# A hybrid decoder step on one core: order of VectorE work at the MoBA gates, order of the operand split, place of the memory transposes

## The reference, cut to what matters

```python
u = jax.nn.sigmoid(g_m) * (h_m @ W['w_proj_m']) + jax.nn.sigmoid(g_a) * (h_a @ W['w_proj_a'])
x = x + u @ W['w_out']
...
# memory_kv: mem is (1, 256, 2048), the keys and values of the cross attention
mn = rms_norm(mem, norm_mem)
return (mn @ w_xk), (mn @ w_xv)
```

## Time and profile before

| | us |
|---|---|
| median of 3 runs | 2289.93 |
| the three runs | 2280.73, 2289.93, 2290.65 |
| the profiled execution | 2281.03 |
| its span, first to last instruction | 2279.5 |
| TensorE busy in the span | 2130.7 (93%) |
| VectorE busy | 1206.3 (53%) |
| ScalarE busy | 797.3 (35%) |
| mean granted TensorE clock | 0.959 |

### The profile page before, as it was taken

One profiled execution on the slowest core, in us unless ns is written; L12 is line 12 of the kernel. 1 busy time (PEld: TensorE's weight loads), 2 busy tenths in 40 slices (PEclk: granted clock), 3 DMA queues, 4 the chain that ended last, 5 costly groups with the idle time before them and its releaser, 6 DMA issues.

```text
span 2279.5 us, 40609 instructions
## 1 busy us (share of the span) xinstructions
PE 2130.7 (93%) x16438; PEld 2009.2 (88%) x16438; DVE 1206.3 (53%) x1424; ACT 797.3 (35%) x1010; POOL 63.5 (3%) x85
## 2 busy tenths in 40 slices
PE   4999997998999999898899877999999999999997
PEld 4989896998778788888899756999999999999997
DVE  4354465343556465656446535666564456666444
ACT  3333332343333333323234333333333333333333
POOL 0011011010000000000000000000000000000000
PEclk7999997999999999999899988999999999999999
DMA  7145434454686876554444451454545555454543
GB/s 244 47 151 175 150 105 140 132 175 145 216 315 244 306 273 219 176 163 147 164 143 157 162 185 37 148 175 157 168 134 173 158 180 183 147 176 144 171 154 115
DMA packets 305491, 384.78 MB, mean 169 GB/s; under 512 B 6146, under 2 KB 278690, under 8 KB 304626
## 3 DMA queue, kind: packets, MB, share of 16 engines
q1 hardware_dynamic: 300530, 365.72, 48.9%
q0 software_dynamic: 4896, 18.13, 2.5%
HBM read 370.94 MB, written 12.88 MB: 168 GB/s over the span
## 4 chain that ended last, share of the span: by engine, by line
PE 87%; DVE 6%; ACT 3%; issue 2%; SPq 1%; DMA 1%; DVEq 0%; POOL 0%; PEldq 0%; ACTq 0%; PEld 0%; POOLq 0%
PE bank L1699 19%; PE bank L1700 19%; PE bank L1703 18%; PE bank L1713 8%; PE bank L1717 6%; PE bank L2158 4%; PE bank L2157 4%; PE bank L2162 4%; ACT w_hi L639 1%; DVE w_lo L1046 1%; PE bank L1710 1%; DVE n_tmp L1078 1%; PE bank L1939 1%; PE bank L1938 1%; PE bank L1942 1%
## 5 line engine op out<-in xcount | busy, mean ns | idle before, releaser
L1699 PE MATMUL bank<-xn_hi,w_hi 128*128 128x288 f32 x3152 | 882.8, 306 | 69.1 <-DVE xn_lo L1086 26.1
L1046 DVE TENSOR_TENSOR w_lo<-raw,w_hi 128x2048 fp32r<-128x2048 f32 (+2 forms) x289 | 605.0, 2096 | 616.7 <-ACT w_hi L639 614.0
L1700 PE MATMUL bank<-xn_lo,w_hi 128*128 128x288 f32 x3152 | 874.1, 303 | 0.0
L639 ACT ACTIVATE w_hi<-raw 128x2048 fp32r<-128x2048 f32 (+2 forms) x289 | 503.9, 1745 | 694.1 <-PE bank L1703 476.7
L1699 PEld LDWEIGHTS bank<-xn_hi,w_hi 128*128 128x128 f32 x3152 | 614.5, 195 | 83.5 <-issue 45.0
L1700 PEld LDWEIGHTS bank<-xn_lo,w_hi 128*128 128x128 f32 x3152 | 614.1, 195 | 0.1
L1703 PE MATMUL bank<-xn_hi,w_lo 128*128 128x288 f32 x3152 | 450.2, 295 | 0.0
L1703 PEld LDWEIGHTS bank<-xn_hi,w_lo 128*128 128x128 f32 x3152 | 429.5, 189 | 0.0
L2157 PE MATMUL bank<-f_hi,w_hi 128*128 128x288 f32 x704 | 191.4, 296 | 0.0
L2158 PE MATMUL bank<-f_lo,w_hi 128*128 128x288 f32 x704 | 190.8, 297 | 0.0
L2157 PEld LDWEIGHTS bank<-f_hi,w_hi 128*128 128x128 f32 x704 | 132.5, 188 | 0.1
(11 more groups left out here) (363 smaller groups left out, 1762.1 us busy)
## 6 DMA issues: line engine op xcount, KB each, us to landing
raw<-w_in_dram SPq DMA_DIRECT2D x44, 2048.0 KB, 9.0
raw<-w_ffn_gate_dram SPq DMA_DIRECT2D x22, 2048.0 KB, 8.1
raw<-w_ffn_up_dram SPq DMA_DIRECT2D x22, 2048.0 KB, 8.1
raw<-w_ffn_down_dram SPq DMA_DIRECT2D x32, 1408.0 KB, 6.6
raw<-cache_k_dram SPq DMA_DIRECT2D x64, 512.0 KB, 5.4
raw<-cache_v_dram SPq DMA_DIRECT2D x64, 512.0 KB, 5.3
raw<-w_out_dram SPq DMA_DIRECT2D x8, 2048.0 KB, 8.6
w_pm_raw<-w_proj_m_dram SPq DMA_DIRECT2D x8, 1024.0 KB, 5.6
```

Of the source, the lines that this page charges most:

```text
L639: nc.scalar.activation(like(wh[ph.half(c)], src), src, ACT.Copy).then_inc(hi_ready, 1)
L1046: nc.vector.tensor_tensor(like(wl[ph.half(c)], src), src, like(wh[ph.half(c)], src).bitcast(F32), ALU.subtract).then_inc(slot_read[ph.slot ...
L1699: mm(out, wh[half][:, k, :], rh[:, k, 0:n], start=k == 0, stop=False)
L1700: mm(out, wh[half][:, k, :], rl[:, k, 0:n], start=False, stop=False)
```

## The change

Three things are moved; no arithmetic is added or removed.

1. `ga_tail` frees the bank right after the multiplication, and stands ahead of `lo` of the same j.
2. At the end of the gates ScalarE splits quarters 0 to 2 of u before it converts the first weight tile of `p_wo`, and VectorE's order becomes: quarters 0 and 1, `ga_tail` of half tile 0, quarter 2, `ga_tail` of half tile 1, first `w_lo`, quarter 3.
3. The memory transposes are made in two groups of 16, one between tiles 2 and 3 and one after tile 3 of the first iteration of `p_wo`; the copies stand between weight conversions, and the loop over the next two iterations is written out.

```diff
 # ScalarE
-            hi(p_wo, 0, 0, 0, src256(p_wo.slot(0), 0))
             for q in range(4):
                 act.wait_ge(x_u, 4 * q + 5)
                 a_copy(xh[:, 4 * q:4 * q + 4, :], U2[:, 4 * q:4 * q + 4, :]).then_inc(x_uhi, 1)
+                if q == 2:
+                    hi(p_wo, 0, 0, 0, src256(p_wo.slot(0), 0))
...
-            for n in (0, 2, 4, 6):
+            def mem_copy(n):
...
-            with act.Fori(1, 3) as i:
-                for j in range(4):
-                    hi(p_wo, i, j // 2, j, src256(p_wo.slot(j // 2), j % 2))
+            for j in range(4):
+                if j < 2:
+                    mem_copy(4 * j)
+                    mem_copy(4 * j + 2)
+                hi(p_wo, 1, j // 2, j, src256(p_wo.slot(j // 2), j % 2))
+            for j in range(4):
+                hi(p_wo, 2, j // 2, j, src256(p_wo.slot(j // 2), j % 2))
 # VectorE
                 dc.run(nc.vector.tensor_tensor(ut[:], G[p_ga.bank(2 + j)][:, 0:NT], sg[:, j, :], ALU.mult))
+                nc.vector.engine_nop().then_inc(evac_done[p_ga.bank(2 + j)], 1)
                 dc.sync()
                 nc.vector.tensor_tensor(U2[:, ds(i * 2 + j, 1), :], U[:, ds(i * 2 + j, 1), :], ut[:].unsqueeze(1), ALU.add).then_inc(x_u, 1)
-                nc.vector.engine_nop().then_inc(evac_done[p_ga.bank(2 + j)], 1)
...
                     if not first:
+                        ga_tail(i - 1, j)
                         lo(p_ga, i, 0, j, src256(p_ga.slot(0), j))
-                        ga_tail(i - 1, j)
...
-            lo(p_wo, 0, 0, 0, src256(p_wo.slot(0), 0))
-            for q in range(4):
-                if q == 3:
-                    ga_tail(7, 0)
-                    ga_tail(7, 1)
+            def u_lo(q):
                 dve.wait_ge(x_uhi, q + 1)
...
+            u_lo(0)
+            u_lo(1)
+            ga_tail(7, 0)
+            u_lo(2)
+            ga_tail(7, 1)
+            lo(p_wo, 0, 0, 0, src256(p_wo.slot(0), 0))
+            u_lo(3)
...
+            for j in range(4):
+                if j < 2:
+                    mem_copy(4 * j + 1)
+                    mem_copy(4 * j + 3)
+                lo(p_wo, 1, j // 2, j, src256(p_wo.slot(j // 2), j % 2))
+                add_to_x(p_wo, (0, 1)[j // 2], (j + 2) % 4, (j + 2) % 4, ds(2 + j, 1))
+            wo_body(2, False)
 # TensorE
+            for j in range(4):
+                tile(p_wo, 0, j // 2, j, j, x_sem=None if j else x_ulo)
+                if j == 2:
+                    pe.wait_ge(landed[2], p_min.landed(0, 0))
+                if j >= 2:
+                    for n in range(4 * j - 8, 4 * j - 4):
+                        mem_rows(n)
             pe.drain().then_inc(slot_read[2], 1)
-            with pe.Fori(1, 3) as i:
+            for i in range(1, 3):
                 for j in range(4):
                     tile(p_wo, i, j // 2, j, j)
```

More of the change, by code:

```diff
@@ L1462, in wo_body, with mem_copy @@
                         add_to_x(p_wo, i - 1, j + 2, j + 2, ds(i * 4 + (j - 2), 1))
-            wo_body(0, True)
-            for n in (1, 3, 5, 7):
+            def mem_copy(n):
                 dve.wait_ge(tp_done, 9 + n + 1)
@@ L1468, in _ @@
                                       B[2 + n % 4][:].rearrange("p (k c) -> p k c", c=P)).then_inc(tp_odd, 1)
-            with dve.Fori(1, 3) as i:
-                wo_body(i, False)
+            wo_body(0, True)
+            for j in range(4):
[5 more added lines that the diff above has]
+            wo_body(2, False)
             def mem_lo(j):
@@ L2020, in _, with mem_rows @@
                 ga_body(i, False)
[L2021 to L2026, removed]
+            def mem_rows(n):
                 t, k4 = n // 4, n % 4
```

## The result

The changed kernel takes 2251.07 us (median of 4 runs, 2247.76 to 2252.39), before beside it 2287.1 (4 runs, 2280.73 to 2290.65): ratio 0.9841, 95% interval 0.9817 to 0.9865, or 36 us (31 to 42). The forecast was 2250, range 2241 to 2264.

The account below looks back on a forecast made before the run. TensorE, busy 93% of the span, bounds it: only its idle or low-clock time can be won. Gates 24.3, projection start 2.2 and transposes 7.2 make 33.7 off 2281.03: 2247 or 2256, forecast 2250, own range 2243 to 2260, wider 2241 to 2264.

Parts of the forecast that it names:

- Gates: Gate stage: with the tail first, the stalls at the iteration edges go; 24.3 us less in all.
- stalls 16.5, clock 5.9 and refill 1.9: Gate stage's sum: TensorE's waits gone, four iterations back from granted clock 0.93, six restarts after a stall saved.
- the second rival: Gates and projection: the clock swings without the stalls, 5.9 + 1.5 + 1.2 us stays, 2256 us; chance 8%.
- the multiplication starts at E - 1.5, right behind the reciprocal: VectorE at a gate edge: multiplication starts 1.5 us before the second half tile's end and takes 0.45.
- The bank is free at E - 1.0: Gate edge: bank released 1.0 us before TensorE ends the second half tile, so the stall goes.
- The weights' cover: Gates' next `w_in` transfer: 3 us of cover for a median transfer, thinnest of the change, costed at nothing.
- The rival of the weights: Gates: shorter iterations find `w_in` missing, 21 us given back, 2268 us at the lower level; chance 12%.
- Start of the projection: Output projection's first tile: TensorE starts 4.2 us earlier but waits for quarter 3; 2.2 us less taken.
- the clock's term: Projection's start: gain 2.7 us if the clock stays up, 1.2 if two new gaps lower it, costing 1.5.
- Memory transposes: Output projection: two groups remove 4.74 us idle and 2.73 of clock and refill, 0.3 added; 7.2 us less.
- The loop: Output projection: writing the loop out costs nothing, since straight-code tiles already stand 6.39 us apart.
- The level: Whole kernel: runs lie on two levels some 9 us apart, so 2247 or 2256 us, equally likely.

Follow-up runs that it names:

- Experiment 1: The kernel before with only the gates' tail order and early bank release changed; ratio 0.9887, median 2262.44 us.
- experiment 2: The kernel before with only the bank's release moved right behind the multiplication, low weights still ahead of the tail; ratio 0.9949, median 2277.2 us.
- experiment 3: The changed kernel with the bank's release put behind the addition again; ratio 0.9867, median 2254.07 us.
- experiment 7: The changed kernel with the next gate weights' transfer held until VectorE has read the first half of the half tiles' weights; median 2259.59 us.
- experiment 6: The changed kernel with TensorE's loop over two iterations of the output projection kept as a loop; ratio 0.9849, median 2251.22 us.
- experiment 4: The kernel before with only the split of u while products run; ratio 0.9971, median 2282.74 us.
- experiment 5: The kernel before with only the memory transposes in two groups of 16, copies between weight conversions; ratio 0.998, median 2283.09 us.
- experiment 9: The changed kernel with VectorE's order at the projection's start: tail 0, quarter 0, tail 1, quarters 1 to 3, low weights last; 2247.75 us, one run.
- experiment 10: The changed kernel with u's low quarter 0 on GpSimd and VectorE's order tail 0, quarter 1, tail 1, quarters 2 and 3, low weights; ratio 0.9832.
- experiment 8: The changed kernel with u's low quarters 0 and 1 made by GpSimd and both tails ahead of VectorE's part of the split; median 2250.1 us.

## Why the prediction was right, point by point

**Gates: 24.3 forecast, 24.22 measured.** Experiment 1 shows that part 1 does it alone. The split into stalls 16.5, clock 5.9 and refill 1.9 is borne out for the clock by experiment 2, where the same instructions with shorter gaps won 5.9 beyond the stalls. (Six times 0.33 is 2.0, not 1.9; what the measured 24.2 leaves beside stalls and clock is 1.8.) "If the low clock of four iterations isn't caused by the gap", the premise of the second rival, is false. The step that failed in a detail is "the multiplication starts at E - 1.5, right behind the reciprocal". The same edge in the changed kernel, VectorE, TensorE and SyncE:

```profile
943.19 1.96 DVE L1343 RECIPROCAL x_gates<-x_gates 128x288 f32<-128x288 f32 x1
945.66 0.46 DVE L1427 TENSOR_TENSOR x_tmp<-bank,x_gates 128x288 f32<-128x288 f32 x1 [0.52 <-DVE x_gates L1343]
```

```profile
946.55 0.30 PE L1713 MATMUL bank<-xn_hi,w_hi 128*128 128x288 f32 x1
```

```profile
952.37 0.37 SPq L437 DMA_DIRECT2D raw<-w_in_dram  x1
```

The next product starts at 946.55, and the last half tile's record ends at 946.72 (E; the records overlap). The reciprocal ends at E - 1.57, as forecast, but the multiplication starts 0.5 behind it, at E - 1.1. "The bank is free at E - 1.0" was really E - 0.6, which is 0.4 ahead of the next product, and with it the early release, which looked like a spare in this stage, is worth 2.4 us (experiment 3). The outcome was the same because 0.4 us was enough. By the same shift the second `lo` ends later, and the next transfer starts at E + 5.65, not E + 5.1.

**The weights' cover** was the thinnest, as said, and held: the list of waits has ScalarE on `w_in` once, 3.2 us at the first edge, as in the earlier trace rows. The next transfers took 8.4 us as a median, not 8.9, and experiment 7 puts the cover at about 3.4 us. The rival of the weights was a real mechanism, not yet in force.

**Start of the projection: 2.2 taken, 3.03 measured** (bounds 1.2 to 2.7). The start at E + 1.75 and the wait for quarter 3 came as forecast, but the gain is larger than either bound. Two things were mis-sized. VectorE's chain was shorter than worked out: second tail, `lo` and quarter 3 ended at E + 4.25, 6.45 and 7.7 instead of 4.45, 6.7 and 8.0, and the tile at E + 11.2 instead of 11.6 (the prediction's own terms give 11.5). The other is the clock's term. In the changed kernel's profile TensorE went over to its lower clock 1.4 us after the restart (matmuls of line 1713 then 0.48 apart instead of 0.27) and reached quarter 3 late, waiting 1.06 us. In the second profile of the same kernel it waited 2.58, at full clock:

```profile
1061.13 0.37 PE L1713 MATMUL bank<-xn_hi,w_hi 128*128 128x288 f32 x1 [1.75 <-DVEq L1428]
...
1067.15 0.40 PE L1713 MATMUL bank<-xn_hi,w_hi 128*128 128x288 f32 x1 [2.58 <-DVE xn_lo L1448]
```

Both resume 6.02 us after the restart, and both tiles end 11.22 to 11.23 behind the half tile. Experiments 6 and 7 have the same gap of 1.75 us at full clock and the same M1 to M2, 8.93 and 8.94. The low clock, while an operand is late, costs nothing here, since it only eats the wait; I had priced it at up to 1.5 us. So the clock did fall behind the new gaps, in one profile of four, and the price was wrong.

**Memory transposes: 7.2 forecast, 6.93 measured.** The idle time behind the second group is 0.26 where 0.3 stood, and the tile behind it is at clock 1.00. Most of the missing 0.3 is a reading of two views as one: 6.99 was taken from TensorE's start in the timeline, 1122.51, to 1129.50 in the chain, which puts the last pass later than the timeline does:

```profile
1129.33 2.27 PE L1703 MATMUL bank<-xn_hi,w_lo 128*128 128x288 f32 x16
```

From timeline to timeline it is 6.82, and the term 4.74 + 2.56 - 0.3 = 7.0.

**The loop** was costed at nothing and gives 0.2 (experiment 6).

**The level** is where the working was wrong, though the number came out. "One is at 2280.73 and two are near 2290", and "the changed kernel is as likely on the one level as on the other" read two levels into four numbers. The 22 runs of before beside experiments 1, 2, 4 and 5 go from 2281.19 to 2295.91, with values all along the way. The marks show where the profiled runs differ: M0 goes from 921.58 to 933.45, through code common to all of them, while the same code gives M0 to M1 alike to 0.2 us. Part of it is the first parameter transfers (2.1 to 8.4 us of TensorE's wait on them). Those with 2.1 to 3.9 reach M0 at 921.58 to 922.87, those with 6.7 to 8.4 at 924.32 to 933.45. What adds the further 6 us in the latest one is not settled: its granted clock from 360 to 460 us is 0.80, where the others have 0.84 to 0.88; its waits on weights ahead of the gates are 1.2 us longer, but experiments 1 and 5 have that too. The forecast of 2250 stood between the two supposed levels and so near the middle of the real spread, 2247.76 to 2258.40 in ten runs of the changed kernel. That it came within 1.1 us of the median was luck; that the three stages give 34.2 us where 33.7 stood was not, though 0.8 too little at the projection stands against 0.4 too much in the other two. The lower end of the range, 2243, is not what its terms give either: 2280.7 less 35.5 is 2245.2.

## What to carry to other kernels

When a consumer's release of a buffer stands behind longer work in the same queue, the price is the stall, the refill of the array and the clock that falls behind it; count all three, and look for edges where the wanted operand had long been there. A split of one wait in two, with a lower clock between them, is harmless as long as a later operand sets the end. To compare two profiles, lay marks around the changed stage before trusting the span: here 5.5 us of 34 were hidden by the start of the program.

## What the runs showed of the hardware

- A gap of 2.20 us on TensorE was followed by its lower clock (1.2 GHz for part of the iteration, granted clock 0.93) in four of six iterations, in the same order in three kernels; a gap of 1.58 us in none of six, but neither was one of 2.79 to 3.52 us at the first edge. Behind the gap at the start of the projection the clock fell in one profile of four with 1.75 us (the changed kernel, not its second profile, nor experiments 6 and 7), with 2.24 us in experiment 4 and not with 2.25 in experiment 3. It fell with shorter ones too, of 1.07 and 0.74 us, in experiment 9. What decides is open.
- An addition on VectorE with both operands in SBUF took 2.75 us instead of 0.46 while GpSimd ran a subtraction of two SBUF operands, and a multiplication with one operand in PSUM took its usual 0.46 beside it. The Trainium skill, "SBUF — State Buffer", section "SBUF: two separate sides", says that VectorE with two SBUF inputs and GpSimd take turns on a shared pair of ports, each for a whole instruction. The trace agrees: the addition ended 0.3 us behind GpSimd's instruction, and with GpSimd idle (experiment 10) it took 0.46 again.
- Where VectorE's next instruction waits for its last result, it stood idle 0.52 us behind the reciprocal in the loop and 0.28 in straight code (experiment 8); behind the multiplication it was 0.16 in the loop and 0.03 in straight code.
